# Mixture of a three-branch layer: the branch loop turned outermost, and seven pairs of gate tiles formed by block products

## What is computed

```
branches = jnp.stack([ret, gla_o, fox_o], axis=2).astype(h.dtype)
y_br = jnp.einsum('bsnw,nwd->bsnd', branches, w_br)
gates = jax.nn.sigmoid(h @ w_mg + b_mg).reshape(b, s, N_BRANCH, D_MODEL)
mixed = jnp.sum(gates * y_br, axis=2) @ w_o
x = x + (gate1[:, None, :] * mixed).astype(x.dtype)
...
u, g = jnp.split(h2 @ w_up, 2, axis=-1)
u = causal_dwconv(u, w_conv, b_conv)
y = (jax.nn.silu(u) * g) @ w_down
```

## Time and profile before

| | us |
|---|---|
| median of 3 runs | 2878.84 |
| lowest, highest | 2878.73, 2879.1 |
| the profiled execution | 2875.43 |
| its span, first to last instruction | 2873.6 |
| PE busy | 2838.0 (99%) |
| DVE busy | 1606.0 (56%) |
| ACT busy | 1176.6 (41%) |
| POOL busy | 1123.3 (39%) |

### The profile page before, as it was taken

One profiled execution on the slowest core, in us unless ns is written; L12 is line 12 of the kernel. 1 busy time (PEld: TensorE's weight loads), 2 busy tenths in 40 slices (PEclk: granted clock), 3 DMA queues, 4 the chain that ended last, 5 costly groups with the idle time before them and its releaser, 6 DMA issues.

```text
span 2873.6 us, 37367 instructions
## 1 busy us (share of the span) xinstructions
PE 2838.0 (99%) x15599; PEld 2397.8 (83%) x15599; DVE 1606.0 (56%) x2244; ACT 1176.6 (41%) x1797; POOL 1123.3 (39%) x461
## 2 busy tenths in 40 slices
PE   8999999999999999999999999999999999999999
PEld 5777888888888877788898988888999877789998
DVE  6444572367675624422266755648668456676683
ACT  4336333342333424532344434444334466443433
POOL 2332345334445332344435344543334423333432
PEclk9999999999999999999999999999999999999999
DMA  8331353346564422233333333333333322233332
GB/s 259 104 103 52 100 194 117 95 141 202 195 200 127 113 80 59 74 96 96 88 101 92 97 107 89 103 96 92 100 110 103 104 67 67 75 93 98 109 103 76
DMA packets 507292, 314.25 MB, mean 109 GB/s; under 512 B 14290, under 2 KB 478836, under 8 KB 506868
## 3 DMA queue, kind: packets, MB, share of 16 engines
q1 hardware_dynamic: 507124, 311.87, 37.0%
HBM read 309.73 MB, written 2.10 MB: 109 GB/s over the span
## 4 chain that ended last, share of the span: by engine, by line
PE 93%; DVE 3%; ACT 1%; DMA 1%; SPq 1%; issue 0%; POOL 0%; DVEq 0%; ACTq 0%
PE b L496 16%; PE b L498 16%; PE b L497 16%; PE o L496 4%; PE o L498 4%; PE o L497 4%; PE s L498 3%; PE s L496 3%; PE s L497 3%; PE b L1226 2%; PE b L1228 2%; PE b L1227 2%; PE s L1226 1%; PE s L1228 1%; PE s L1227 1%; PE b L1164 1%
## 5 line engine op out<-in xcount | busy, mean ns | idle before, releaser
L3376 POOL TENSOR_TENSOR lo<-raw,hi 128x1024 fp32r<-128x1024 f32 (+2 forms) x451 | 1121.0, 2496 | 1721.1 <-ACT hi L1503 1371.8
L1503 ACT ACTIVATE hi<-raw 128x1024 fp32r<-128x1024 f32 (+2 forms) x454 | 464.5, 1035 | 318.7 <-DMA raw<-in_w_up_dram 92.9
L496 PE MATMUL b<-HH,hi 128*128 128x512 f32 x1296 | 517.7, 399 | 0.0
L498 PE MATMUL b<-HH,lo 128*128 128x512 f32 x1296 | 505.2, 390 | 0.0
L497 PE MATMUL b<-HL,hi 128*128 128x512 f32 x1296 | 505.1, 390 | 0.0
L496 PEld LDWEIGHTS b<-HH,hi 128*128 128x128 f32 x1296 | 243.3, 188 | 57.9 <-issue 7.1
L498 PEld LDWEIGHTS b<-HH,lo 128*128 128x128 f32 x1296 | 243.3, 188 | 51.9
L497 PEld LDWEIGHTS b<-HL,hi 128*128 128x128 f32 x1296 | 243.5, 188 | 50.2 <-issue 1.4
L2526 DVE SCALAR_TENSOR_TENSOR AA<-raw,CA,AA 128x512 f32<-128x512 f32 x140 | 143.5, 1025 | 3.5
L496 PE MATMUL b<-FH,hi 128*128 128x512 f32 (+1 forms) x385 | 141.7, 368 | 0.9 <-POOL lo L3376 0.9
L497 PE MATMUL b<-FL,hi 128*128 128x512 f32 (+1 forms) x385 | 141.3, 367 | 0.0
(11 more groups left out here) (654 smaller groups left out, 6837.9 us busy)
## 6 DMA issues: line engine op xcount, KB each, us to landing
raw<-in_w_up_dram SPq DMA_DIRECT2D x88, 512.0 KB, 4.1
raw<-in_w_ada_dram SPq DMA_DIRECT2D x80, 512.0 KB, 4.9
raw<-in_w_in_dram SPq DMA_DIRECT2D x76, 512.0 KB, 4.1
raw<-in_w_mg_dram SPq DMA_DIRECT2D x48, 512.0 KB, 3.8
raw<-in_ffn_w_gate_dram SPq DMA_DIRECT2D x44, 512.0 KB, 3.9
raw<-in_ffn_w_up_dram SPq DMA_DIRECT2D x44, 512.0 KB, 3.9
raw<-in_w_down_dram SPq DMA_DIRECT2D x32, 448.0 KB, 3.8
raw<-in_ffn_w_down_dram SPq DMA_DIRECT2D x32, 448.0 KB, 3.9
```

The costliest lines, as they stand in the source:

```text
L496: e.matmul(out, wh, xh, start=start and k == 0, stop=False)
L498: mm = e.matmul(out, wl, xh, start=False, stop=stop and k == last)
L1503: e.activation(t["hi"][:, c % NSLOT, 0:w], K.raw[:, c % NSLOT, 0:w], ACT.Copy).then_inc(*m.hi.up(c))
L3376: e.tensor_tensor(t["lo"][:, s, 0:w], K.raw[:, s, 0:w], t["hi"][:, s, 0:w].bitcast(F32), ALU.subtract).then_inc(*m.lo.up(n))
```

## The change

The mixture's loops are exchanged: the branch is now the outer loop (order 0, 2, 1: retention, forgetting, gated linear attention) and the tile pair the inner one. Units are numbered f = 0 to 11. The sums over the branches therefore stay open for all eight output tiles, so `MX` has eight tiles, and `MH` and `ML` are formed in units 8 to 11 (their tiles lie turned by four places). For units 5 to 11 of each layer the two gate tiles are formed by the same seven half products as in the feed-forward stages, in buffers of their own (`mTH`, `mTL`, `mTR`, `mEH`, `mEL`, `mER`, `mMP`) that lie over dead ones. There is one block of `mEH`, `mEL`, `mER`, not two: the sums of a pair wait until the pair before it has done H5. `halves_whole` stands ahead of unit 2 on DVE, `halves_sums` ahead of unit 3, the split of the halves in units 3 and 4. The mixture uses six PSUM banks in place of four from unit 2 on. The filler has 28 steps as before, but in units 4 to 11 only the two branch products of a unit yield, so it advances one chunk per unit there; before it advanced three chunks per unit and was done in the fifth.

```diff
-            (5, 6, 7, 8, 9, 10, 12, 13, 14, 15, 16, 17, 19, 20))
+            (5, 6, 7, 8, 9, 10, 12, 13, 14, 15, 16, 17, 19, 20),
+            (5, 6, 7, 8, 9, 10, 11), (5, 6, 7, 8, 9, 10, 11))
+MIX_BRANCHES = (0, 2, 1)
...
-        fill = chain(P.gated(l, 0), P.mixing(l, 0, (0, 2)))
+        fill = chain(P.gated(l, 0), P.mixing(l, (0, 1)))
         weave(P.gla_attention(l), fill)
         drain(beside(P.gated(l, 1), ada, 8))
+        P.order = BIG6
+        drain(beside(P.mixing(l, range(2, 12)), ada, 28))
         P.order = BIG4
-        drain(beside(chain(P.mixing(l, 0, (1,)), *[P.mixing(l, dp, (0, 2, 1)) for dp in (1, 2, 3)]), ada, 28))
...
+        for f in units:
+            n, dp = MIX_BRANCHES[f // 4], f % 4
+            keys = [("mg", l, 2 * dp + u, n) for u in range(2)]
+            if f in PAIRS_OF[4 + l]:
+                c0 = n * 1024 + dp * 256
+                yield from self.pair(4 + l, f, (wmg, c0), (wmg, c0 + 128), m.atake.at(*keys[0]), m.atake.at(*keys[1]))
+            else:
+                for u, key in enumerate(keys):
+                    for _ in self.project(wmg, n * 1024 + (2 * dp + u) * 128, key, lambda key=key: m.atake.at(*key)):
+                        yield BUSY if f == 4 else None
...
+            if f == 2:
+                self.halves_whole(i)
+            if f == 3:
+                self.halves_sums(i)
+            if f == 4:
+                q.wait_ge(m.dense.at("br", l, 7, 0))
+            if f in PAIRS_OF[i]:
+                self.next_chunk()
+                self.next_chunk()
+                yield BUSY
+                yield BUSY
+                if g is not None:
+                    self.pair_sums(i, g)
+                yield BUSY
+                self.pair_out(i, f, 0)
+                yield BUSY
+                self.pair_out(i, f, 1)
+                if g is not None:
+                    self.pair_low(i, g, 0)
...
-        before = pair_before(i, f, 2)
+        before = pair_before(i, f, 2 if i < 4 else 1)
         q.wait_ge(m.dense.at("block", i, before) if before is not None else None)
...
-        area("MX", 10, [128, 2, S])
+        area("MX", 20, [128, 8, S])
```

More of the change, by code:

```diff
@@ L284, in block, with sums_of @@
         b = pair_block(i, f)
-        return tuple(self.t[x][:, b, :, :] for x in ("EH", "EL", "ER"))
+        return tuple(self.t[x][:, b, :, :] for x in (("EH", "EL", "ER") if i < 4 else ("mEH", "mEL", "mER")))
+    def sums_of(self, i, j):
+        t = self.t
+        if i < 4:
+            return t["TH"][:, j, :, :], t["TL"][:, j, :, :], t["TR"][:, j, :, :]
+        return t[f"mTH{j}"][:, :, :], t["mTL"][:, j, :, :], t["mTR"][:, j, :, :]
     def loaded(self, n):
@@ L1143, in out_proj @@
         halves = WHOLE[nid]
-        place = (lambda k: (LAST + k) % ROOM) if name in ("w_down", "ffn_w_down") else (lambda k: k)
+        place = ((lambda k: (LAST + k) % ROOM) if name in ("w_down", "ffn_w_down") else
+                 (lambda k: (k + 4) % 8) if name == "w_o" else (lambda k: k))
         def entries(d):
@@ L1213, in ffn @@
             else:
-                yield from self.pair(i, f, up_freed)
+                yield from self.pair(i, f, (wu, cu + f * 128), (wg, cg + f * 128), up_freed(f), m.vtake.at("gateup", i, f))
             if f in DOWN:
@@ L1230, in half_product, with pair @@
             mm.then_inc(*m.dense.up(*keys))
-    def pair(self, i, f, up_freed):
+    def pair(self, i, f, above, below, up_freed, gate_freed):
         m, t, K = self.m, self.t, self.K
-        wu, cu, wg, cg, _ = ffn_weights(self.I, i)
-        na = self.weight(wu, 0, 8, cu + f * 128, 128)
-        nb = self.weight(wg, 0, 8, cg + f * 128, 128)
+        up, gate = pair_keys(i, f)
+        na = self.weight(above[0], 0, 8, above[1], 128)
+        nb = self.weight(below[0], 0, 8, below[1], 128)
         assert nb == na + 1
@@ L1931, in mixing @@
             yield None
[L1932 to L1934 removed]
+            for d in (2 * dp, 2 * dp + 1) if n == 1 else ():
+                q.wait_ge(m.vtake.at("mixed", l, d, 1))
+                p = (d + 4) % 8
+                e.activation(t["MH"][:, p, :], t["MX"][:, p, :], ACT.Copy).then_inc(*m.atake.up(("mh", l, d)))
     def out_proj(self, name, i, norm):
@@ L2005, in ffn_jobs, with halves_high @@
             self.ffn_silu(i, f)
-    def halves_high(self, i):
+    def halves_high(self, i, js=range(4)):
         e, q, m, t = self.e, self.q, self.m, self.t
-        for j in range(4):
+        for j in js:
+            high, _, whole = self.K.sums_of(i, j)
             q.wait_ge(m.vtake.at("traw", i, j))
-            e.activation(t["TH"][:, j, :, :], t["TR"][:, j, :, :], ACT.Copy).then_inc(*m.atake.up(("t", i, j)))
+            e.activation(high, whole, ACT.Copy).then_inc(*m.atake.up(("t", i, j)))
     def pair_high(self, i, f, part):
@@ L2032, in pair_copies @@
         e, q, m, t, K = self.e, self.q, self.m, self.t, self.K
-        A, G = [self.bank[K.where.get((x, i, f), "b0")] for x in ("mid", "gateup")]
+        A, G = [self.bank[K.where.get(key, "b0")] for key in (("mid", i, f), pair_keys(i, f)[1])]
+        MP = t["MP" if i < 4 else "mMP"]
         g = pair_before(i, f, 1)
@@ L2813, in gated, with mixing, branch @@
                 *m.vtake.up(("gated", l, which, h)))
-    def mixing(self, l, dp, branches):
+    def mixing(self, l, units):
         e, q, m, t = self.e, self.q, self.m, self.t
         SG, MX = t["SG"], t["MX"]
-        for n in branches:
-            for u in range(2):
-                yield from self.tile()
-            self.next_chunk()
-            for u in range(2):
+        i = 4 + l
+        for f in units:
+            n, dp = MIX_BRANCHES[f // 4], f % 4
+            g = f + 1 if f + 1 in PAIRS_OF[i] else None
+            def branch(u):
                 d = 2 * dp + u
-                yield None
+                p = (d + 4) % 8
                 out = self.out_of(("br", l, d, n))
@@ L3549, in places @@
         area("GT", 45, [128, 4, S])
-        area("MH", 36, [128, 8, S], F32R)
+        area("MH", 28, [128, 8, S], F32R)
         area("ML", 20, [128, 8, S], F32R)
+        area("MX", 20, [128, 8, S])
         area("SG", 8, [128, 2, S])
-        area("MX", 10, [128, 2, S])
+        area("mMP", 8, [128, 3, 256])
+        area("mTL", 36, [128, 4, 4, 256], F32R)
+        area("mTR", 36, [128, 4, 4, 256])
+        for j, tile in enumerate((44, 46, 10, 12)):
+            area(f"mTH{j}", tile, [128, 4, 256], F32R)
+        area("mEH", 14, [128, 1, 3, 512], F32R)
+        area("mEL", 17, [128, 1, 3, 512], F32R)
+        area("mER", 17, [128, 1, 3, 512])
         area("FH", 0, [128, ROOM, S], F32R)
```

148 lines of the change are left out of this document (101 added, 47 removed).

## The result

The changed kernel takes 2881.95 us (median of 20 runs, 2878.38 to 2885.09); the kernel before, in 20 runs, 2877.1 (2875.07 to 2879.1, and one run far off at 3338.28, which hardly moves the median). The ratio is 1.0016 with a 95% interval of 1.0009 to 1.0023: slower by about 5 us, clear of noise, and still within the 0.2% that the prediction called no change. The forecast was 2880.5.

The account below looks back on a forecast made before the run. PE, busy 99% of the span, was taken to bound the kernel. -11.2 + 5.7 + 1.4 + 0.3 + 3.0 + 1.8 + 0.7 = +1.7 us, added to the median 2878.84, gave 2880.5 us; 8-in-10 range 2870 to 2893.

Parts of the forecast that it names:

- PE's work: Both layers' mixtures: 14 pairs of gate tiles as half products save 0.80 us each, 11.2 us less.
- layer 0, fold: PE waits 5.7 us for the filler's reduction, queued on DVE behind the halves' sums; lower end 1.5.
- clock behind it: After the fold's wait in layer 0 a stretch at lower granted clock costs PE 1.4 us, between 0 and 2.8.
- unit 3: Layer 0: PE waits 0.3 us for the branch chunk, held up by the halves' sums; between 0 and 1.
- unit 5: Layer 0's first pair: waits for the second gate chunk and `mEL` cost 3.0 us, between 0 and 4.1.
- units 6 to 11, layer 0: With one block, `mEL` comes slightly late for H5: 1.8 us in all, between 0 and 14.
- w_o's third chunk: End of layer 0's mixture: the chunk waits for H7 of unit 11, costing 0.7 us, between 0 and 1.5.
- layer 1: Layer 1's mixture: `mEL` is ready at 13.2 against 14.08 us, so 0 lost; other end 7 us.
- Rival 1: The cover holds: the fold costs 1.5 us and all else nothing, 2869 us; chance 0.13.
- rival 2: The single block binds in layer 0: units 6 to 11 lose 14 us, unit 5 4.1, 2894 us; chance 0.27.
- Rival 3: Clock granted low more than once: fold and first pair each cost 2.8 us, 2885 us; chance 0.10.

Follow-up runs that it names:

- e2: The changed kernel with the halves' four 1024-column sums put behind the reduction for the filler's fold in DVE's queue: 2878.74 us, 1.0004.
- e6: The changed kernel with 16 of layer 0's 28 filler steps made earlier, the last 12 from unit 6 on, bank counter set back: 2877.53 us, 1.0002.
- e9: The changed kernel with layer 0's pairs in units 9 to 11 only, its halves in units 6 to 8, bank counter set back: 2871.57 us, 0.9980.
- e11: The changed kernel with pairs in layer 1 alone, bank counter set back, second gate chunk's low part ahead of the product with the gate: 2872.14 us, 0.9982.
- e1: The changed kernel with PE's bank counter set back by 7 behind each layer's mixture: 2881.24 us, 1.0012.
- e4: The changed kernel with the 7 pairs in layer 1 alone and no halves in layer 0: 2888.15 us, 1.0033.
- e7: The kernel before, with PE's bank counter moved on by 7 behind layer 1's mixture, no pairs, no exchange: 2890.51 us, 1.0049.
- e8: The changed kernel with the 7 pairs in layer 0 alone, bank counter set back by 7, no halves in layer 1: 2886.06 us, 1.0032.

## Why the prediction was right, and where it was not

It was right in sign and range, and its forecast, 2880.5, lies 1.5 us under the measured median; a good part of that agreement is luck. The forecast was a rise of 1.7 us; the profiled execution rose by 3.84, the medians by 4.85. The rise was put on a median of three runs, 2878.84, that lies 1.74 above the median of twenty, and some errors in the terms cancel. The terms, in the prediction's order (read one by one, so they don't add up to the last tenths):

| term | forecast | in the trace after |
|---|---|---|
| PE's work | -11.2 | -10.9: 14 x 0.78; the product behind a pair takes 0.03 us more |
| layer 0, fold | 5.7 | 5.5 (a wait of 5.36, the fold at 378.33 against 372.95) |
| clock behind it | 1.4 | 1.8 (7.23 - 5.44) |
| unit 3 | 0.3 | 0 |
| unit 5 | 3.0 | 4.0 (7.33 - 5.44 = 1.9, and 12.17 - 10.08 = 2.1) |
| units 6 to 11, layer 0 | 1.8 | 0.1 |
| w_o's third chunk | 0.7 | 0.8 (a wait of 0.77), 1.2 with what stands around it |
| layer 1 | 0 | 1.0, all of it in unit 11 |
| from w_o to layer 1's mixture | no term | -0.35 |
| behind layer 1's mixture | no term | 1.9 |

- **The fold** is the step that carried the forecast, and it held to 0.2 us. In its detail it was off: the sums took 6.82 us, not 9.03, since POOL's second operation (372.37 to 375.48) met the filler's accumulation, which took 3.61 instead of 1.53. Sums and accumulations together were put at 10.56 us and took 10.43: what the collisions cost in all came out, only another instruction paid. Rival 1, which had the fold's wait at 1.5, is out. e2 shows that this is where the time went, and that the prediction's next step, unit 3, was only hidden by the fold's own wait: with that gone its 0 became 3.3.
- **The clock** behind the fold has the right sign, but the size of its term, 1.4 us against 1.8 measured, is luck. It came from one window of 3.6 us at the start of the program, which is the tail of a longer stretch. The two windows ahead of it in before:

```profile
16.00:20.00 4.00, 2.03 (x10) 2.03 (x10) 2.93 (x4) 3.63 (x5) 0.00 (x0) 0.57 1.12 336
20.00:24.00 4.00, 4.00 (x20) 2.21 (x23) 2.67 (x4) 1.21 (x2) 0.00 (x0) 0.50 1.10 348
```

  Counted over all three in the same way, the term would have been 5.1 us.
- **Unit 5** came as argued, first the gate chunk that waits for the filler's slot and POOL, then `mEL` on the late DVE, near the upper end of 4.1. e6 and e9 show the filler to be the cause.
- **One block for all pairs**, rival 2, didn't bind: the count of 14.2 us against a cover of 14.08 was too high by at least that 0.1, since no unit from 6 to 11 waits in layer 0. Where it did bind, in unit 11 of layer 1, the prediction had 0: it left out that SP by then issues the chunks of `w_o`, whose low part follows on POOL right behind the branch chunk's. e11 shows that the order on DVE decides it: with the low part one place earlier the wait is gone.
- **The step that is missing** in the prediction is the banks. The prediction counted what the change adds to each queue, but not that a pair takes three banks where two tiles took two. The stages behind it kept their instructions and lost 1.6 us to it (a wait for `X` that e1 takes away), and it could have been far worse: with 7 in place of 14 it is 13 us (e4, e7). That the changed kernel has pairs in both layers, 14 in all, is its luck.
- **Rival 3**, the clock granted low more than once, got 0.10 with the argument that unit 5's wait is split in two. Of the four traces with that wait (the changed kernel, e1, e2, e8) two show the second fall, at 1.5 us. So it looks less like one case out of several than like a chance in each execution, and by this 0.10 was too low. The medians rise 1 us more than the profiled execution did, which fits, but how often the other executions fell isn't on record.
